# A bank of turned probabilities per job in both attention mixers of a two-block transformer kernel

## The chip, the cores and the metric

The kernel runs on one core of a Trainium2 chip. The metric is the device time of one execution in microseconds (us); lower is better. The engines named are TensorE (PE, matmuls; PEld is its weight loading), VectorE (DVE), ScalarE (ACT), GpSimd (POOL), and SyncE (SP), which issues the DMAs.

## The reference, cut to what matters

Two blocks of a transformer are computed one after the other on 256 tokens, in float32. The first block has two layers and carries 256 context tokens beside the 256 latent ones. Each layer is a half feed-forward, a mixer, and another half feed-forward. The change is in the two mixers of this first block, the "even" one (layer 0) and the "odd" one (layer 1).

```
# even mixer: 8 heads of latent attention beside a convolution of width 31 over 512 channels
att_c = context_attention(q_c, k_c, v_c)              # context queries over the 256 context keys
att_l = latent_attention(q_l, k_l, v_l, k_c, v_c)     # latent queries over context and latent keys, 512
y = a * sigmoid(g)                                    # for both token sets
y = depthwise_conv(y, width=31) + bias
y = layer_norm(y, g, b)                               # over the 512 channels
conv = silu(y)
out = concat([att, conv]) @ w_out

# odd mixer: 8 heads with 2 shared key heads, and 8 heads with a bias table by neighbourhood
s = q @ k.T * scale (+ bias)                          # 512 keys
p = softmax(s)
o = p @ v
```

## The kernel before, in words

The program is a list of blocks; in each, every engine has its own instruction stream, written out in order in the code, and semaphores (the tallies `t[...]`) join them. There is no scheduler: the order on an engine is the order of its Python code.

The attention of a mixer is a pipeline of 32 jobs. A job is one tile of 128 queries of one head; jobs 2h and 2h+1 are the two query tiles of head pair h. In `even_mixer` (line 1250) jobs 0 to 15 are the context's, over 256 keys, and jobs 16 to 31 the latents', over 512. In `odd_mixer` (line 1911) all have 512 keys; jobs 0 to 15 use the shared key heads and run between chunks of the input projection, jobs 16 to 31 add a bias by a second matmul. A job passes through these operations:

- `logits(j)` on PE (L1498; odd L2121, and L2130 with L2131 for the bias), into one of a few PSUM banks; it waits until `exponents` of the job that used the bank before is done.
- `maximum(j)` on DVE (L1811, L2315), `exponents(j)` on ACT (L1659, L2195), and on DVE `scaling_of(j)` (a reciprocal of the row sum, L1815, and a multiplication, L1817; odd L2302, L2304).
- `turn_probs(j)` on PE (L1507, L2098): transposes of the probabilities into PSUM, two for 256 keys, four for 512.
- a copy of the turned probabilities of both jobs of a pair from PSUM to SBUF. In the even mixer ACT makes it (`copy_probs`, L1666); over 512 keys a pair fills banks 4 and 5 together. In the odd mixer the pair always fills both banks, and ACT (`copy_even`, L2202) and DVE (`copy_odd`, L2311) copy half each.
- `weigh(h)` on PE (L1519, L2112), the product with the values, then `place(h)` on ACT (L1672, L2207).

The loop over slots sets the order. In slot s of the even mixer PE does turn_probs of job s-3, then weigh of a pair where one is due, then logits of job s. DVE does scaling_of job s-2, then maximum of job s, then some taps. ACT does the copy that is due, then exponents of job s.

The even mixer's convolution is 124 taps on DVE (L1778, one for each of 4 channel tiles and 31 positions), of which `TAPS_OF_UNIT` gives numbers to the seven units of the input projection and `TAPS_OF_STEP` to the steps of the loop. When all are done, its layer norm runs between the jobs: the mean over channels by four matmuls (L1567) in slot 16, its subtraction on DVE (L1872), the squares on ACT (L1737), the variance by 16 matmuls of one column (L1573) in slot 20, root on ACT (L1740) and reciprocal on DVE (L1875) on 4 columns, the spreading of the result over the partitions by four matmuls (L1579) in slot 22, the scaling on DVE (L1879), and the Silu on ACT (L1745) near the end. In two slots (`HEAD_AHEAD`) the first two weight units of the output projection are split into parts, ACT making the first (L511) and DVE the second (L519).

In the odd mixer SP loads tables of the bias in small pieces (L2001): those of heads 2 and 3 when the last norm of the input projection is done, those of heads 4 to 7 behind them and after the logits of job 15. DVE adds a mask to each (`mask`, L2298) at fixed steps, ahead of the scaling and maximum of that step.

After each mixer the output projection (L533) begins with parts of the mixed rows, split by ACT (L589) and DVE (L620).

## Time and profile before

| | us |
|---|---|
| median of 3 runs | 3458.52 (3452.37 to 3458.77) |
| the profiled execution | 3456.14 |
| its span | 3454.4 |
| PE busy in the span | 3246.7 (94%) |
| DVE busy | 1983.7 (57%) |
| ACT busy | 1410.2 (41%) |
| mean granted clock of TensorE | 0.969 of full speed |

The span is what the trace covers; the 1.7 us around it are start and end. Busy times are of one execution. Two matmuls in a row overlap at their ends, so the step from one start to the next is the cost of one, not the duration shown. float32 matmuls show as two rows each. A granted clock of 1.00 is 2.4 GHz, of 0.50 is 1.2 GHz.

### The profile page before, as it was taken

Reading aid. Unit: us, or ns where it says so; the run is one execution under the profiler, and the core shown is the slowest. Engines: PE = TensorE matmul, PEld = TensorE weight load, DVE = VectorE, ACT = ScalarE, POOL = GpSimd, SP = SyncE. Lnnn points to the kernel's source line nnn. Section 1 sums busy time; section 2 is a strip of 40 time slices with the busy share of each in tenths; the row PEclk is TensorE's granted clock in tenths of the full one; section 3 lists DMA queues with packets and bytes.
Section 4 is the critical chain, followed back from the end, with each engine's and each line's share of the span. In section 5 each row is a group of like instructions: output and inputs, shape, how many; then the busy total and the mean of one; then the engine's idle time right before and its main releaser. Section 6 shows DMA issues by size and latency. Waiting matters only on the chain. (4 is left out here: it accounts for less than half of the span.)

```text
span 3454.4 us, 51012 instructions
## 1 busy us (share of the span) xinstructions
PE 3246.7 (94%) x20326; PEld 2879.2 (83%) x20326; DVE 1983.7 (57%) x2557; ACT 1410.2 (41%) x2310; POOL 191.7 (6%) x151
## 2 busy tenths in 40 slices
PE   5999999789999999999889999999999999999999
PEld 4878777457787788887569999899999999999898
DVE  4776758537767733335555555566455555655654
ACT  3333335333333322224345444446444444454443
POOL 1000011000000100011000000200000102100000
PEclk8999999899999999999999999999999999999999
DMA  7566532015666433332226656554456565543564
GB/s 223 160 177 186 162 87 77 11 42 160 175 188 171 131 90 99 94 108 79 57 63 172 175 158 189 154 170 110 145 149 186 168 183 159 162 134 108 164 187 128
DMA packets 769419, 478.27 MB, mean 138 GB/s; under 512 B 37973, under 2 KB 746164, under 8 KB 769092
## 3 DMA queue, kind: packets, MB, share of 16 engines
q1 hardware_dynamic: 767200, 474.88, 48.5%
q8 instruction: 137, 2.24, 0.3%
q10 hardware_dynamic: 2020, 0.64, 0.1%
q14 instruction: 62, 0.51, 0.1%
HBM read 474.40 MB, written 1.05 MB: 138 GB/s over the span
## 5 line engine op out<-in xcount | busy, mean ns | idle before, releaser
L533 PE MATMUL psum<-normed,weights_part 128*128 128x256 f32 (+1 forms) x11616 | 1827.5, 319 | 39.5 <-DVE normed L808 11.6
L533 PEld LDWEIGHTS psum<-normed,weights_part 128*128 128x128 f32 x11616 | 1654.5, 193 | 197.3 <-issue 43.0
L519 DVE TENSOR_TENSOR weights_part<-weights,weights_part 128x2048 fp32r<-128x2048 f32 (+1 forms) x413 | 885.9, 2147 | 618.7 <-ACT weights_part L511 618.4
L511 ACT ACTIVATE weights_part<-weights 128x2048 fp32r<-128x2048 f32 (+1 forms) x413 | 738.5, 1791 | 654.3 <-PE psum L533 415.0
L533 PE MATMUL psum<-hidden,weights_part 128*128 128x256 f32 (+1 forms) x4224 | 680.7, 323 | 0.3 <-DVE hidden L821 0.3
L533 PEld LDWEIGHTS psum<-hidden,weights_part 128*128 128x128 f32 x4224 | 614.5, 190 | 61.8 <-DVE hidden L821 0.6
L1003 DVE SCALAR_TENSOR_TENSOR stage<-weights,cond,stage 128x768 f32<-128x768 f32 x294 | 281.1, 1020 | 0.0
L406 POOL TENSOR_TENSOR square<-square,rinvs 128x256 f32<-128x256 f32 (+1 forms) x39 | 65.1, 1669 | 2830.3 <-ACT rinvs L391 2828.7
L725 ACT ACTIVATE rinvs<-psum 128x256 f32<-128x256 f32 (+1 forms) x88 | 39.8, 452 | 210.6 <-PE psum L533 210.5
L533 PE MATMUL psum<-weights_part,normed 128*128 128x256 f32 x960 | 121.6, 287 | 0.0
L533 PEld LDWEIGHTS psum<-weights_part,normed 128*128 128x128 f32 x960 | 117.0, 192 | 4.9 <-issue 4.8
L727 ACT ACTIVATE hidden<-rinvs 128x256 f32 (+3 forms) x88 | 43.9, 499 | 177.0 <-DVE rinvs L819 177.0
L836 DVE SCALAR_TENSOR_TENSOR x<-psum,gate,x 128x256 f32<-128x256 f32 (+1 forms) x112 | 49.6, 479 | 113.2 <-PE psum L533 113.2
L727 ACT ACTIVATE hidden<-roots 128x256 f32 (+3 forms) x88 | 43.9, 499 | 173.0 <-DVE roots L819 173.0
L725 ACT ACTIVATE roots<-psum 128x256 f32<-128x256 f32 (+1 forms) x88 | 39.9, 454 | 177.6 <-PE psum L533 177.5
L819 DVE TENSOR_TENSOR rinvs<-rinvs,psum 128x256 f32<-128x256 f32 (+1 forms) x88 | 45.4, 516 | 97.2 <-ACT rinvs L725 97.2
L1778 DVE SCALAR_TENSOR_TENSOR mix<-ypad,vec,mix 128x512 f32<-128x512 f32 x120 | 87.1, 774 | 0.5
L819 DVE TENSOR_TENSOR roots<-roots,psum 128x256 f32<-128x256 f32 (+1 forms) x88 | 45.4, 516 | 63.5 <-ACT roots L725 63.5
L821 DVE TENSOR_TENSOR hidden<-rinvs,hidden 128x256 f32 (+3 forms) x88 | 46.3, 526 | 60.8 <-ACT hidden L727 60.8
L821 DVE TENSOR_TENSOR hidden<-roots,hidden 128x256 f32 (+3 forms) x88 | 46.3, 526 | 60.8 <-ACT hidden L727 60.8
L533 PE MATMUL psum<-mixed_part,weights_part 128*128 128x512 f32 (+1 forms) x384 | 70.1, 347 | 4.7 <-DVE mixed_part L620 4.7
L533 PEld LDWEIGHTS psum<-mixed_part,weights_part 128*128 128x128 f32 x384 | 61.7, 198 | 13.4 <-issue 5.6
(445 smaller groups left out, 2450.2 us busy)
## 6 DMA issues: line engine op xcount, KB each, us to landing
weights<-in_l_ffn_w_in SPq DMA_DIRECT2D x176, 512.0 KB, 5.2
weights<-in_ffn_w_gu SPq DMA_DIRECT2D x176, 512.0 KB, 4.9
weights<-in_l_mod_w SPq DMA_DIRECT2D x168, 384.0 KB, 3.4
weights<-in_w_in SPq DMA_DIRECT2D x34, 1024.0 KB, 5.2
weights<-in_w_gate SPq DMA_DIRECT2D x64, 512.0 KB, 5.2
weights<-in_l_ffn_w_out SPq DMA_DIRECT2D x64, 384.0 KB, 4.1
weights<-in_ffn_w_down SPq DMA_DIRECT2D x64, 384.0 KB, 3.9
weights<-in_l_ffn_w_out SPq DMA_DIRECT2D x64, 320.0 KB, 3.3
```

The costliest lines, as they stand in the source:

```text
L406: k.nc.gpsimd.tensor_tensor(total, total, buffers[n % 2], ALU.add).then_inc(summed.sem, 1)
L511: k.nc.scalar.activation(k.parts[part][0][:, W], k.slots[slot][:, W], ACT.Copy).then_inc(k.high_done, 1)
L519: k.nc.vector.tensor_tensor(k.parts[part][1][:, W], k.slots[slot][:, W], k.parts[part][0][:, W].bitcast(F32), ALU.subtract).then_inc(k.spl ...
L533: mm = k.nc.tensor.matmul(to, left[a], right[b], start=first and n == 0, stop=last and n == len(PASSES) - 1)
L725: nc.scalar.activation(row[:, T], k.psum[:, bank(spec, c), T], ACT.Silu).then_inc(t["silu_done"].sem, 1)
L727: nc.scalar.activation(one(k.hidden[0], i * RING + c, col=T), row[:, T], ACT.Copy)\
L819: nc.vector.tensor_tensor(row, row, k.psum[:, bank(spec, c) + 1, T], ALU.mult).then_inc(t["gated"].sem, 1)
L821: nc.vector.tensor_tensor(one(k.hidden[1], i * RING + c, col=T), row, one(k.hidden[0], i * RING + c, col=T).bitcast(F32), ALU.subtract)\
L836: last = nc.vector.scalar_tensor_tensor(row, k.psum[:, bank(spec, c), part], gate(chunk, cond) if callable(gate) else gate, row, ALU.mult, ...
L1003: ins = k.nc.vector.scalar_tensor_tensor(total, self.buffer(n), scale, total, ALU.mult, ALU.add)
L1778: last = nc.vector.scalar_tensor_tensor(total, of, weight, total, ALU.mult, ALU.add)
```

## The change

The pair of jobs no longer shares its copy. `turned_bank` takes a job: job j's turned probabilities go to bank 4 + j % 2, four tiles of 128 columns fill it exactly. `copy_probs(j)` on ACT copies one job's, in both mixers; the odd mixer's copy on DVE is gone. turn_probs(j) waits for the copy of job j-2. In a slot PE does the logits first, then turn_probs, then weigh; ACT does the copy, the exponents and only then `place`, a slot later than before. A slot is added at the end.

In the even mixer the taps are dealt anew: the units of the projection take 77 of the 124 (67 before), slots 0 to 2 two each and slots 3 to 15 one each (two each up to slot 14 before). The mean moves to slot 17, the variance to slot 22. The variance is now four matmuls of 512 columns against a matrix of 1/512, so that every partition gets it, and the spreading matmuls are gone; root (ACT) and reciprocal (DVE) work on 128x512 instead of 128x4, in slot 23. The Silus move behind the last exponents, and the two weight splits to slots 28 and 31.

```diff
-TAPS_OF_UNIT = (8, 10, 12, 11, 11, 13, 2)
-TAPS_OF_STEP = (2,) * HEAD_LOGITS + (2,) * 15
-CONV_MEAN, CONV_VARIANCE, CONV_SPREAD = 16, 20, 22
-HEAD_AHEAD = {24: 0, 27: 1}
+TAPS_OF_UNIT = (11, 13, 13, 13, 12, 13, 2)
+TAPS_OF_STEP = (2,) * (HEAD_LOGITS + 3) + (1,) * 16
+CONV_MEAN, CONV_VARIANCE, CONV_SCALED = 17, 22, 23
+HEAD_AHEAD = {28: 0, 31: 1}
...
-    def turned_bank(h):
-        if 2 * h < N_CONTEXT:
-            return k.psum[:, 4 + h % 2, :].rearrange("p (n q) -> p n q", q=LAT)
-        return k.psum[:, 4:6, :].rearrange("p b (n q) -> p (b n) q", q=LAT)
+    def turned_bank(j):
+        return k.psum[:, 4 + j % 2, :].rearrange("p (n q) -> p n q", q=P)[:, 0:len(key_tiles(j // 2)), :]
...
             def turn_probs(j):
                 pe.wait_ge(t["scaling"].sem, t["scaling"].base + j + 1)
-                h, qt = j // 2, j % 2
-                if qt == 0 and h:
-                    pe.wait_ge(t["copied"].sem, t["copied"].base + max(h - 1 if j < N_CONTEXT else h, 0))
...
+                if j >= 2:
+                    pe.wait_ge(t["copied"].sem, t["copied"].base + j - 1)
...
             def weigh(h):
-                pe.wait_ge(t["copied"].sem, t["copied"].base + h + 1)
+                pe.wait_ge(t["copied"].sem, t["copied"].base + 2 * h + 2)
...
+                if 0 <= s < N_HEAD_JOBS:
+                    logits(s)
...
                 for j in range(N_HEAD_JOBS):
                     if s == turn_slot(j):
                         turn_probs(j)
                 for h in range(N_HEAD_JOBS // 2):
                     if s == turn_slot(2 * h + 1) + 1:
                         weigh(h)
-                if 0 <= s < N_HEAD_JOBS:
-                    logits(s)
...
                 if s == CONV_VARIANCE:
-                    pe.wait_ge(t["conv_squared"].sem, t["conv_squared"].base + n_conv)
-                    for b in range(4):
-                        for c in range(n_conv):
-                            mm = nc.tensor.matmul(k.psum[:, 1, b:b + 1], conv_squares[c][:, b * P:(b + 1) * P], k.const("ones")[:, 0:1],
-                                                  start=c == 0, stop=c == n_conv - 1)
+                    for c in range(n_conv):
+                        pe.wait_ge(t["conv_squared"].sem, t["conv_squared"].base + c + 1)
+                        mm = nc.tensor.matmul(k.psum[:, 1, :], k.const("mean512"), conv_squares[c], start=c == 0, stop=c == n_conv - 1)
                     mm.then_inc(t["conv_variance"].sem, 1)
-                if s == CONV_SPREAD:
...
-            def copy_probs(h):
-                act.wait_ge(t["probs_turned"].sem, t["probs_turned"].base + 2 * h + 2)
+            def copy_probs(j):
+                h, qt = j // 2, j % 2
+                act.wait_ge(t["probs_turned"].sem, t["probs_turned"].base + j + 1)
                 if h >= 2:
                     act.wait_ge(t["weighted"].sem, t["weighted"].base + h - 1)
-                nc.scalar.activation(turned_probs[h % 2][:, 0:len(key_tiles(h)), :], turned_bank(h), ACT.Copy).then_inc(t["copied"].sem, 1)
+                nc.scalar.activation(turned_probs[h % 2][:, 0:len(key_tiles(h)), qt * P:(qt + 1) * P], turned_bank(j), ACT.Copy)\
+                    .then_inc(t["copied"].sem, 1)
...
+                if s >= N_HEAD_JOBS:
+                    for c in ((0,), (1, 2), (3,), (), ())[s - N_HEAD_JOBS]:
+                        gate_conv(c)
+            place(N_HEAD_JOBS // 2 - 1)
...
-                if s == CONV_VARIANCE + 1:
+                if s == CONV_SCALED:
                     dve.wait_ge(t["conv_root"].sem, t["conv_root"].base + 1)
-                    nc.vector.reciprocal(k.rms[:, 1, 0:4], k.rms[:, 0, 0:4]).then_inc(t["conv_inverse"].sem, 1)
+                    nc.vector.reciprocal(conv_inverse, conv_inverse).then_inc(t["conv_inverse"].sem, 1)
...
-            def copy_odd(h):
-                dve.wait_ge(t["probs_turned"].sem, t["probs_turned"].base + 2 * h + 2)
-                if h >= 2:
-                    dve.wait_ge(t["weighted"].sem, t["weighted"].base + h - 1)
-                nc.vector.tensor_copy(turned_probs[h % 2][:, 2:4, :], PT[:, 2:4, :]).then_inc(t["odd_copied"].sem, 1)
```

In the order of PE in the even mixer, from the variance on, before. Rows with `consts,weights` are turn_probs, with `head_rows` weigh, with `head_keys` logits; x4 counts calls.

```order
L1573 MATMUL psum<-consts,rinvs 128x1 x2
L1507 MATMUL psum<-consts,weights 128x128 x4
L1519 MATMUL psum<-head_rows_3953,head_values_3952 64x256 x4
L1498 MATMUL psum<-head_keys_3966,head_queries_3967 128x512
L1507 MATMUL psum<-consts,weights 128x128 x4
L1498 MATMUL psum<-head_keys_3966,head_queries_3967 128x512
L1579 MATMUL psum<-consts,rms 128x128 x4
L1507 MATMUL psum<-consts,weights 128x128 x4
```

The same place now:

```order
L1497 MATMUL psum<-head_keys_3966,head_queries_3967 128x512
L1505 MATMUL psum<-consts,weights 128x128 x4
L1570 MATMUL psum<-square,consts 128x512 x2
L1570 MATMUL psum<-rinvs,consts 128x512 x2
L1497 MATMUL psum<-head_keys_3966,head_queries_3967 128x512
L1505 MATMUL psum<-consts,weights 128x128 x4
L1517 MATMUL psum<-head_rows_3953,head_values_3952 64x256 x4
```

The logits of a slot now stand ahead of its transposes and of weigh, so a logits call stands between the copy of a pair and the weigh that needs it; the row of L1579 is gone.

On ACT in the even mixer around the root of the layer norm, before (`rinvs<-mix` is a square, `head_rows` the copy, `weights,head_rowsum` the exponents):

```order
L1659 ACTIVATE weights,head_rowsum_3964<-psum,head_negmax_3963 128x512
L1740 ACT_TABLE_LOAD
L1740 ACTIVATE rms<-psum,eps 128x4
L1666 ACTIVATE head_rows_3953<-psum 128x1024
L1659 ACT_TABLE_LOAD
L1659 ACTIVATE weights,head_rowsum_3964<-psum,head_negmax_3963 128x512
L1672 ACTIVATE mix_3950<-psum 64x256 x2
L1659 ACTIVATE weights,head_rowsum_3964<-psum,head_negmax_3963 128x512
```

Now:

```order
L1649 ACTIVATE weights,head_rowsum_3964<-psum,head_negmax_3963 128x512
L1737 ACT_TABLE_LOAD
L1737 ACTIVATE roots<-psum,eps 128x512
L1657 ACTIVATE head_rows_3953<-psum 128x4x128
L1649 ACT_TABLE_LOAD
L1649 ACTIVATE weights,head_rowsum_3964<-psum,head_negmax_3963 128x512
L1668 ACTIVATE mix_3950<-psum 64x256 x2
L1657 ACTIVATE head_rows_3953<-psum 128x4x128
```

A copy of 1024 columns for each pair has become one of 512 for each job, and the number of table loads at the root is the same.

On DVE in the odd mixer at the last masks, before (`odd_negmax` is the maximum, `weights` the scaling, `COPY` the copy of half a pair):

```order
L2298 TENSOR_TENSOR shared_queries_12105<-shared_queries_12105,consts 128x256 x2
L2302 RECIPROCAL odd_inverse_12115<-odd_rowsum_12114 128x1
L2304 TENSOR_SCALAR weights<-weights,odd_inverse_12115 128x512
L2311 COPY turned_probs_12111<-psum 128x512
L2315 TENSOR_REDUCE odd_negmax_12113<-psum 128x1
L2298 TENSOR_TENSOR shared_queries_12105<-shared_queries_12105,consts 128x256 x2
```

Now:

```order
L2296 TENSOR_TENSOR shared_queries_12152<-shared_queries_12152,consts 128x256 x2
L2300 RECIPROCAL odd_inverse_12162<-odd_rowsum_12161 128x1
L2302 TENSOR_SCALAR weights<-weights,odd_inverse_12162 128x512
L2307 TENSOR_REDUCE odd_negmax_12160<-psum 128x1
L2296 TENSOR_TENSOR shared_queries_12152<-shared_queries_12152,consts 128x256 x2
```

The copy between scaling and maximum is gone from DVE.

## Rows read from the trace of the kernel before

**Rows 1.** Windows: stretch, length; busy (count) of PE, PEld, DVE, ACT, POOL; PEclk, DMA, GB/s.

```profile
602.26:644.52 42.26, 29.23 (x96) 15.82 (x94) 34.58 (x79) 17.67 (x49) 0.23 (x1) 0.76 0.08 26
644.52:729.14 84.62, 60.97 (x219) 33.93 (x218) 30.63 (x63) 37.73 (x68) 0.00 (x0) 0.84 0.00 0
1622.61:1687.55 64.94, 64.54 (x394) 49.11 (x393) 33.35 (x52) 27.80 (x47) 0.00 (x0) 1.00 0.22 64
```

**Rows 2.** Timeline, PE, first mixer, 256 keys: start, duration, what, count, idle before and its releaser.

```profile
608.86 0.69 PE L1507 MATMUL psum<-consts,weights 128*128 128x128 f32 x2 [4.25 <-DVE weights L1817]
...
619.50 1.08 PE L1519 MATMUL psum<-head_rows,head_values 128*64 128x256 f32 x4
620.51 0.70 PE L1498 MATMUL psum<-head_keys,head_queries 96*128 96x256 f32 x2
```

**Rows 3.** Timeline of DVE, first mixer, the same jobs.

```profile
610.84 0.42 DVE L1811 TENSOR_REDUCE head_negmax<-psum 128x1 f32<-128x256 f32 x1
611.17 1.41 DVE L1778 SCALAR_TENSOR_TENSOR mix<-ypad,vec,mix 128x512 f32<-128x512 f32 x2
...
612.95 0.42 DVE L1811 TENSOR_REDUCE head_negmax<-psum 128x1 f32<-128x256 f32 x1
```

**Rows 4.** Timeline of PE, first mixer, jobs over 512 keys and the end.

```profile
644.52 3.60 PE L1567 MATMUL psum<-mix,consts 128*128 128x512 f32 x8
...
659.99 0.61 PE L1573 MATMUL psum<-consts,square 128*128 128x1 f32 x4 [2.91 <-ACT rinvs L1737]
...
703.90 1.12 PE L1507 MATMUL psum<-consts,weights 128*128 128x128 f32 x4 [5.02 <-DVE weights L1817]
...
729.14 6.17 PE L533 MATMUL psum<-mixed_part,weights_part 128*128 128x512 f32 x19 [2.60 <-DVE mixed_part L620]
```

**Rows 5.** Timeline of ACT, second mixer: root, tables.

```profile
1649.51 0.60 ACT L2177 ACTIVATE near_values<-psum 128x512 f32<-128x512 f32 x1 [1.37 <-PE psum L533]
1650.12 1.28 ACT L2189 ACT_TABLE_LOAD   x1
1651.42 0.69 ACT L2189 ACTIVATE rinvs<-psum,eps 128x512 f32<-128x512 f32 x1
```

**Rows 6.** Timeline of DVE, second mixer: reciprocal of a whole tile.

```profile
1652.27 3.34 DVE L2263 RECIPROCAL rinvs<-rinvs 128x512 f32<-128x512 f32 x1
```

**Rows 7.** Timeline of PE, second mixer: one pair of jobs late in its loop.

```profile
1735.05 0.63 PE L2098 MATMUL psum<-consts,weights 128*128 128x128 f32 x4 [0.40 <-ACT turned_probs L2202]
1735.61 1.94 PE L2112 MATMUL psum<-turned_probs,near_values 128*64 128x256 f32 x8
1737.48 1.13 PE L2130 MATMUL psum<-near_keys,near_queries 128*128 128x512 f32 x2
...
1738.87 0.60 PE L2098 MATMUL psum<-consts,weights 128*128 128x128 f32 x4
1739.31 1.02 PE L2130 MATMUL psum<-near_keys,near_queries 128*128 128x512 f32 x2
1740.17 0.59 PE L2131 MATMUL psum<-shared_queries,consts 128*128 128x256 f32 x2
1741.16 0.63 PE L2098 MATMUL psum<-consts,weights 128*128 128x128 f32 x4 [0.40 <-ACT stage L2202]
```

**Rows 8.** Timeline of SP and DVE, second mixer: the bias tables.

```profile
1688.15 0.69 DVE L2311 COPY stage<-psum 128x512 f32<-128x512 f32 x1
...
1693.09 10.35 SPq L2001 DMA_DIRECT2D roots<-in_l_na_rpb  x16
...
1716.69 0.76 DVE L2298 TENSOR_TENSOR shared_queries<-shared_queries,consts 128x256 f32<-128x256 f32 x2 [5.60 <-DMA shared_queries<-in_l_na_rpb]
```

**Rows 9.** Timeline of PE, second mixer: after the bias wait, and the end.

```profile
1718.10 1.12 PE L2098 MATMUL psum<-consts,weights 128*128 128x128 f32 x4 [6.01 <-DVE weights L2304]
...
1767.49 17.77 PE L533 MATMUL psum<-mixed_part,weights_part 128*128 128x256 f32 x134 [2.12 <-DVE mixed_part L620]
```

**Rows 10.** Timeline of DVE, first mixer: taps before a weight split.

```profile
519.68 2.29 DVE L519 TENSOR_TENSOR weights_part<-weights,weights_part 128x2048 fp32r<-128x2048 f32 x1 [1.89 <-ACT weights_part L511]
```

More of the change, by code:

```diff
@@ L1299, in even_mixer @@
     tap_before = {(c, n): tap_place[c, n - 1] for c, n in TAPS if n}
-    slots = HEAD_LOGITS + N_HEAD_JOBS + HEAD_LAG + 1
+    conv_inverse = k.roots[:, 0, :]
+    slots = HEAD_LOGITS + N_HEAD_JOBS + HEAD_LAG + 2
     def bank_rows(u):
@@ L1552, in _ @@
                     head_step(f)
+                if 0 <= s < N_HEAD_JOBS:
+                    logits(s)
+                for g in range(len(GROUPS)):
+                    if f == TURNED_AT[g]:
+                        turn_group(g)
                 for j in range(N_HEAD_JOBS):
@@ L1558, in _ @@
                         weigh(h)
-                if 0 <= s < N_HEAD_JOBS:
-                    logits(s)
-                for g in range(len(GROUPS)):
-                    if f == TURNED_AT[g]:
-                        turn_group(g)
                 if s == CONV_MEAN:
@@ L1724, in _ @@
                         evict_group(n)
-                for h in range(N_HEAD_JOBS // 2):
-                    if s == turn_slot(2 * h + 1):
-                        copy_probs(h)
-                    if s == turn_slot(2 * h + 1) + 1 and h % 2:
-                        place(h)
+                for j in range(N_HEAD_JOBS):
+                    if s == turn_slot(j):
+                        copy_probs(j)
                 if 0 <= s < N_HEAD_JOBS:
                     exponents(s)
+                for h in range(1, N_HEAD_JOBS // 2, 2):
+                    if s == turn_slot(2 * h + 1) + 2 and h < N_HEAD_JOBS // 2 - 1:
+                        place(h)
                 if s in HEAD_AHEAD:
@@ L1943, in odd_mixer @@
     chunks = {FIRST_CHUNK + n: chunk for n, chunk in enumerate(CHUNKS)}
[L1944 removed]
+    last_step = FIRST_LOGITS + turn_slot(N_JOBS - 1) + 2
     parts_of_tokens = halves(TOK)
@@ L1986, in head, with turned_bank @@
         return (j % N_SHARED) // 2
-    PT, O = k.psum[:, 4:6, :].rearrange("p b (n q) -> p (b n) q", q=LAT), k.psum[:, 6, :]
+    def turned_bank(j):
+        return k.psum[:, 4 + j % 2, :].rearrange("p (n q) -> p n q", q=P)
+    O = k.psum[:, 6, :]
     spread_bank = (4, 5, 6, 7, 7, 7, 7, 7, 7)
@@ L2157, in _ @@
                         turn_heads(g)
+                if 0 <= s < N_JOBS:
+                    logits(s)
                 for j in range(N_JOBS):
@@ L2163, in _ @@
                         weigh(h)
-                if 0 <= s < N_JOBS:
-                    logits(s)
         @block.scalar
@@ L2242, in _ @@
                     root(ROOTS_AT[f])
-                for h in range(N_JOBS // 2):
-                    if s == turn_slot(2 * h + 1):
-                        copy_even(h)
-                    if s == turn_slot(2 * h + 1) + 1 and h % 2:
-                        place(h)
+                for j in range(N_JOBS):
+                    if s == turn_slot(j):
+                        copy_probs(j)
                 if 0 <= s < N_JOBS:
                     exponents(s)
+                for h in range(1, N_JOBS // 2, 2):
+                    if s == turn_slot(2 * h + 1) + 2:
+                        place(h)
         @block.vector
@@ L2359, in _ @@
                         scaling_of(j)
-                for h in range(N_JOBS // 2):
-                    if s == turn_slot(2 * h + 1):
-                        copy_odd(h)
                 if 0 <= s < N_JOBS:
```

62 lines of the change are left out of this document (26 added, 36 removed).

## The prediction

> **What bounds the kernel now.** I read the page first. PE is busy 94% of the span, so only places where PE waits or runs at a low clock can give much. The 40 slices show two such places, at the ends of the two attention loops, and the windows around them give the sizes. In the first mixer PE is busy 29.23 us of 42.26 while the context's jobs run, at a mean clock of 0.76, and 60.97 of 84.62 us in the rest, at 0.84 [rows 1]. A mean of 0.76 is 1.2 GHz for about half of the stretch. The early part of the second mixer is another case: PE busy 64.54 of 64.94 us at full clock, covered by the projection's chunks. There the order inside a slot is worth nothing. What ends PE's waits stands in the timelines. At the start it waits 4.25 us for the first scaling, behind DVE's taps [rows 2]. DVE takes 2.11 us from one maximum to the next, with two taps that last 1.41 together [rows 3]. Over 512 keys PE waits for the squares of the layer norm, 2.91 us, and for a scaling queued behind a weight split, 5.02 us [rows 4]. Late in the second mixer every pair shows a 0.40 us wait for a copy, and 6.11 us from pair to pair [rows 7]; once, PE waits 6.01 us, because DVE waits 5.60 us for bias tables [rows 8, 9]. Neither ACT nor DVE is full over 512 keys (37.73 and 30.63 of 84.62 us [rows 1]). Both loops end in a chain to the output projection, which starts at 729.14 and 1767.49 [rows 4, 9], and what follows is mostly PE, so I let a shift of these two starts count fully.
>
> **Prices at full clock**, start to start: logits over 512 keys 0.86, four transposes 0.44, weigh over 512 keys 1.87, bias matmul half of the logits, 0.43 [rows 7]; weigh over 256 keys 1.01 [rows 2]. Logits and transposes over 256 keys I take as half, 0.43 and 0.22.
>
> **First mixer, projection.** Ten taps move into the units, at 0.7 us (half of 1.41 [rows 3]) 7 us. Before the weight split DVE stands idle, 1.89 us at the third unit [rows 10], and no unit gets more than three taps more, 2.1 us. PE needs that split only a unit later. Cost 0; without that cover at most the 7 us.
>
> **First mixer, context jobs.** The start stays: the first scaling still stands behind the same taps, and the maximum of job 3 stays at 610.84 [rows 3]. From slot 3 on DVE has one tap: 2.11 - 0.7 = 1.4, I take 1.45 us a slot. PE needs 0.43 + 0.22 + 0.5 = 1.2 at full clock, 2.4 at half. At full clock DVE sets the pace and the maximum of job 16 is at 610.84 + 13 x 1.45 = 629.7; at half clock PE does, 13 x 2.4 = 31.2, at 642.0. I assume one cold spell of about 3.5 slots at the start, since the 4.25 us wait remains: 3.5 x 0.95 = 3.3, so 633.0, logits of job 16 at 632.3.
>
> **First mixer, jobs over 512 keys.** With the copy made a slot ahead of its weigh, and two banks, PE should run without the copy's waits. ACT needs for a job about 0.7 for the exponents, 0.6 for the copy and 0.4 for place, less than PE's 2.24 (0.86 + 0.44 + 0.94). Sum on PE for slots 16 to 27: 12 logits 10.3, transposes of jobs 13 to 24 4.6, weigh 6 to 11 9.5, mean and variance 8 matmuls of 0.86 6.9, and 0.1 a slot for gaps 1.2: 32.5. To this comes one new wait. Counted from the logits of job 22, the variance ends at 4.7, the exponents of job 23 at 7.4, table load 1.28 and root 0.69 [rows 5] 9.4, and the reciprocal of a whole tile takes 3.34 [rows 6] where 4 columns took almost nothing: 12.8. The scaling of job 22 stands behind it on DVE and is done at 13.3; PE comes to its transposes at 10.1. It waits 3.2. Together 35.7. Bounds of this wait: 0 if PE is late anyway, 5 if the root is.
> Slots 28 to 35: 4 logits 3.4, 7 turns 3.1, 4 weighs 7.5, so 14.0. The split in slot 28 lasts 1.9 on ACT and 2.29 on DVE [rows 10] and holds the next scaling; PE has one slot of slack and waits 1.9. The one in slot 31 holds the scaling of job 30 with fewer jobs left to cover it: 4.4 (5.02 before [rows 4]). The last copy before the last weigh 0.7. Together 21.0. Moving the Silus costs nothing: three of them and their table load, about 3.2 us of ACT, lie beside the 4.4 wait.
> For cold PE after the waits of 3.2 and 4.4 I add 2.5 + 3.0. The last weigh ends at 632.3 + 35.7 + 21.0 + 5.5 = 694.5, and the projection starts 2.6 later [rows 4], at 697.1 instead of 729.14: -32.0. The removed parts (the wait of 2.91, 16 small matmuls, the spreading and its wait) are within this difference.
>
> Where the page's rule would change this: the row shows a table load of 1.28 behind an ACT instruction that has just ended, and the root starting 1.30 after the load's start [rows 5]. The Trainium skill, page "ScalarE: Activation LUTs", section "What ACT_TABLE_LOAD costs", says that a switch costs the load and then a drain of about 1.38 us, 2.66 in all. By that rule the reciprocal would end 1.4 later and the wait be 4.6 instead of 3.2. The trace does not agree, so the sum keeps 1.28.
>
> **Second mixer.** Until 1687.55 nothing. Then DVE does one copy fewer (0.69, 0.6 net [rows 8]) ahead of the last norm, after which SP issues the bias tables at 1693.09; their landing, 23.6 later at 1716.69, holds DVE, and through it PE until 1718.10 [rows 8, 9]. So this point moves by 0.6 only, to 1717.5, whatever PE does before it. One logits call is moved ahead of the wait. After it: transposes of 15 jobs 6.6, 11 logits with bias 14.2, 8 weighs 15.0, together 35.8, 0.3 of gaps, 0.9 for the last copy, 2.5 for a cold start as before: 39.5. The last weigh ends at 1757.0, the projection starts 2.1 later at 1759.1, against 1767.49: -8.4. Bounds: nothing gained beyond the 0.6, or 2.5 more if the start is warm.
>
> **Sum.** 32.0 + 8.4 = 40.4. 3456.14 - 40.4 = 3415.7 for the profiled execution, which lies 2.4 below the median of the runs shown and inside their spread. I forecast 3416.
>
> **Rivals.**
> 1. Same mechanism, warmer: PE is so dense that it stays at 2.4 GHz through both loops. Then 3.3 + 5.5 + 2.5 fall away: 3405. For it: late in the second mixer PE kept full clock in a loop with a 0.40 us wait per pair. Against it: the waits of 4.25 and 6.0 us remain [rows 2, 9], and the clock fell with such: four transposes last 1.12 behind the 6.01 wait, 0.63 elsewhere [rows 7, 9].
> 2. New waits take half of it: the layer norm's chain (variance, root, 3.34 us reciprocal) and the splits each stall the in-order DVE and ACT longer than I worked out, since ACT's copy now stands ahead of every exponents and itself waits for PE's transposes. Price: some 8 us more in the full-key part, 4 to 5 us of cold PE with it, and the context jobs at 638 rather than 633: 3416 + 17 = 3433. For it: half of PE's waits before were for scaling on DVE [rows 2, 4]. Against it: three slots lie between exponents and transposes.
> 3. Slower: the clock. If short gaps at every bank change keep TensorE at 1.2 GHz through both loops, the context jobs end at 642.0; the work after them, 32.5 + 14.0 = 46.5, takes 93 with the splits hidden, so the projection starts at 738, 9 later than now; the second mixer's 35.8 take 72, and its projection starts 25 later. Together 3490. It decides when about half of the some 100 us of PE work in the loops runs at 1.2 GHz beyond what I assumed, as each such microsecond costs one more. Against it: the mean clock in the sparser loop of now is 0.76 and 0.84 [rows 1], not 0.5.
> The Trainium skill, page "TensorE: Matmul & The Clock Gate", section "A second HAM failure mode: psum-queue depth-cycling", tells of this: cycling through PSUM banks every iteration gives PE small idle times between groups, and its clock goes back and forth. The rows late in the second mixer, gaps of 0.40 without such a fall, speak against it here.
> 4. It does not do what it says: the waits for copies were only a cover for DVE's pace, and PE now waits for scaling instead, with the reciprocal's 3.34 and the later tail paying the rest back: 3456. For it: DVE's 34.58 busy of 42.26 us in the context part [rows 1]. Against it: the taps removed there are DVE's.
>
> **Chances.** The forecast 0.58 (its own range 3409 to 3426), rival 1 0.15, rival 2 0.21, rival 3 0.04, rival 4 0.02. The range 3403 to 3438 takes in rivals 1 and 2 nearly whole and the bounds of the new waits. A measurement of this kernel can tell 0.2%, 7 us, from no change. Faster by more than that holds in the first three cases, 0.94; slower in rival 3, 0.04; within it in rival 4, 0.02.
>
> **What would show it.** Right: maxima in slots 3 to 15 of the first mixer about 1.45 us apart once the clock is up; PE busy over 80% from job 16 on, no wait of transposes for a copy, a wait of about 3 us behind the 128x512 reciprocal and one of about 4 behind the second split; the projections starting near 697 and 1727 (1759 less the 32 before); a pair in the second mixer every 5.3 to 5.5 us; the bias landing still the longest wait there. Wrong: PEclk near 0.5 through the loops, scaling waits of several us per pair, or PE waiting for weight splits in the first mixer's projection.

## The result

| | before | after |
|---|---|---|
| median, us (lowest to highest) | 3456.1 (3452.4 to 3458.8), 4 runs | 3420.5 (3417.3 to 3425.9), 4 runs |
| ratio, 95% interval | | 0.9899 (0.988 to 0.9918) |
| profiled execution, its span | 3456.14, 3454.4 | 3425.85, 3424.1 |

The changed kernel is 1% faster. Its profiled execution is the slowest of its four, so stretches are compared below, not spans. The first fence has the windows of the changed kernel that answer to [rows 1]: the context jobs, the jobs over 512 keys with the way to the projection, and the second mixer from turn(17) to its projection.

```profile
607.29:636.50 29.21, 25.59 (x104) 14.57 (x102) 27.21 (x71) 18.70 (x58) 0.00 (x0) 0.88 0.11 37
636.50:698.66 62.16, 49.55 (x179) 25.84 (x179) 31.62 (x59) 38.32 (x76) 0.00 (x0) 0.92 0.00 0
1687.32:1731.91 44.59, 40.03 (x169) 24.11 (x169) 19.21 (x49) 22.07 (x55) 0.00 (x0) 0.94 0.00 1
```

The context jobs take 29.21 us instead of 42.26, the next stretch 62.16 instead of 84.62, the last 44.59 instead of the 49.39 between the two rows of [rows 9]. PE is busy 88% and 80% of the first two, and its mean clock rose from 0.76 and 0.84 to 0.88 and 0.92. The timeline of DVE, over 256 keys, answers to [rows 3]:

```profile
624.35 0.42 DVE L1807 TENSOR_REDUCE head_negmax<-psum 128x1 f32<-128x256 f32 x1
624.68 0.74 DVE L1774 SCALAR_TENSOR_TENSOR mix<-ypad,vec,mix 128x512 f32<-128x512 f32 x1
...
625.80 0.41 DVE L1807 TENSOR_REDUCE head_negmax<-psum 128x1 f32<-128x256 f32 x1
```

One tap stands between two maxima that are 1.45 us apart, not two and 2.11. The timeline of PE over 512 keys answers to [rows 4]:

```profile
661.77 1.01 PE L1505 MATMUL psum<-consts,weights 128*128 128x128 f32 x4 [3.06 <-DVE weights L1813]
...
678.96 1.12 PE L1505 MATMUL psum<-consts,weights 128*128 128x128 f32 x4 [2.64 <-DVE weights L1813]
...
688.66 0.66 PE L1505 MATMUL psum<-consts,weights 128*128 128x128 f32 x4 [3.62 <-DVE weights L1813]
...
694.12 1.94 PE L1517 MATMUL psum<-head_rows,head_values 128*64 128x256 f32 x8 [0.69 <-ACT head_rows L1657]
...
698.66 0.70 PE L533 MATMUL psum<-mixed_part,weights_part 128*128 128x512 f32 x2 [2.60 <-DVE mixed_part L620]
```

Three waits for a scaling are left, behind the reciprocal and behind each weight split; no transposes wait for a copy. In the second mixer, what answers to [rows 7, 9]:

```profile
1687.32 1.12 PE L2095 MATMUL psum<-consts,weights 128*128 128x128 f32 x4 [7.87 <-DVE weights L2302]
...
1697.77 1.94 PE L2108 MATMUL psum<-stage,near_values 128*64 128x256 f32 x8
...
1703.74 1.91 PE L2108 MATMUL psum<-turned_probs,near_values 128*64 128x256 f32 x8 [0.38 <-ACT x L2204]
...
1709.23 1.94 PE L2108 MATMUL psum<-stage,near_values 128*64 128x256 f32 x8
...
1724.66 1.91 PE L2108 MATMUL psum<-turned_probs,near_values 128*64 128x256 f32 x8 [1.00 <-ACT x L2204]
...
1731.91 0.36 PE L533 MATMUL psum<-mixed_part,weights_part 128*128 128x256 f32 x1 [2.12 <-DVE mixed_part L620]
```

From weigh to weigh it is 5.97 and 5.49 us in turn, against 6.11 before. Each longer one holds a wait that was not there before, for ACT's `place`.

**Where the time went, by stretches.** A runs from the first head step to the layer norm's mean, B from there to the first mixer's output projection, C from the last spreading of the second mixer (1657.05, before 1687.55) to its projection. Each length is the difference of two starts on PE. The last four kernels come from the experiments.

| kernel | A | B | C | median, us | ratio to before (95%) |
|---|---|---|---|---|---|
| before | 80.01 | 84.62 | 79.94 | | |
| after | 68.84 | 62.16 | 74.86 | 3420.5 | 0.9899 (0.988 to 0.9918) |
| first mixer only | 68.79 | 62.13 | 79.91 | 3428.9 | 0.9921 (0.9905 to 0.9938) |
| second mixer only | 78.26 | 83.03 | 74.54 | 3447.9 | 0.9984 (0.9973 to 0.9995) |
| before, logits first | 72.91 | 74.54 | 74.94 | 3435.8 | 0.9944 (0.9929 to 0.9959) |
| after, logits last | 74.53 | 72.53 | 80.49 | 3444.0 | 0.9968 (0.9958 to 0.9978) |

Before and after differ by 38.7 us in these three stretches (11.2, 22.5, 5.1). What lies outside them differs by chance: the mixer starts at 483.53 instead of 480.36 in code that is the same, and in the fourteen kernels profiled for this text that start lies between 477.3 and 483.5; between the first projection and the last spreading it is 958.4 us in both; from the second projection to the end it is 1685 to 1696 us in all of them (1686.9 before, 1692.2 after).

How far can one trace be trusted for one stretch? The changed code repeats well: in the four kernels that have its first mixer unaltered, A is 68.52 to 68.84 and B 61.87 to 62.16, and in the seven with its second mixer C is 74.54 to 74.92. The old first mixer was traced twice and repeats less well: the second-mixer kernel, which has it too, shows A and B 1.75 and 1.6 shorter than before. Measured against that trace, the gain of the first mixer is 30.3 us and not 33.6, and that of the three stretches 35.4 and not 38.7, which is nearer to the 35.6 between the medians. So gains counted from before in A and B may be some 2 us too large in each; differences between changed kernels are not touched by this.

### The profile page after: what moved, and what is told of

It is laid out like the page before. It is cut to its first block and busy times, and to the rows that moved or that the text cites. A ratio compares the mean times of both kernels' runs of the same rounds, so it can differ in the third digit from the quotient of the medians.

```text
span 3424.1 us, 51000 instructions
## 1 busy us (share of the span) xinstructions
PE 3239.0 (95%) x20294; PEld 2878.2 (84%) x20294; DVE 1977.5 (58%) x2541; ACT 1420.1 (41%) x2342; POOL 193.0 (6%) x151
```

## The experiments

Medians in one set of runs are compared with before in the same set (3454.4, 3458.5, 3454.1, 3453.5); the ratios account for that, so two kernels of different sets are compared by their ratios (0.001 is 3.5 us). Stretches are those of the table.

**1. The two mixers apart.** The diff's part on one mixer was taken, that on the other left out.

> Only the second mixer's part of the change, on the kernel before. Theory (the two mixers' gains add, each where the two traces show it): the first mixer is as before (84.6 us from its mean to the output projection), the second mixer's stretch from turn(17) to its projection takes 44.6 us instead of 49.4, and the time is 5 us below before, near 3451. Rival (part of the second mixer's gain comes from what the first mixer's change leaves behind, or from nothing but the shift of a run): less than 2 us.

> Only the first mixer's part of the change: the second mixer as before. Theory: the output projection of the first mixer starts 30 to 34 us earlier than before, the second mixer keeps its pairs of 6.11 us and 49.4 us from turn(17) to its projection; the time is 31 us below before, near 3425, that is 5 us above the changed kernel. Rival: the second mixer's part cost something elsewhere and this kernel is as fast as the changed one, 3420.

Measured: 0.9984 and 0.9921, whose product is 0.9905 against 0.9899 for both. From turn(17) to the projection 44.75 us with the second mixer's part alone; with the first mixer's alone its A and B are those of the changed kernel within 0.05 and C that of before. The gains add, and the first mixer has 33.6 of 38.7 us. The time of the first-mixer kernel, 3428.9, is above the 3425 that I expected: by its ratio it is 27 us below before (21 to 33), where I expected 31. That fits the 30.3 us of the other trace of the old first mixer better than the 33.6.

**2. The taps.**

```
-TAPS_OF_UNIT = (11, 13, 13, 13, 12, 13, 2)
-TAPS_OF_STEP = (2,) * (HEAD_LOGITS + 3) + (1,) * 16
+TAPS_OF_UNIT = (8, 10, 12, 11, 11, 13, 2)
+TAPS_OF_STEP = (2,) * HEAD_LOGITS + (2,) * 15
```

with the old order of `TAPS`.

> The changed kernel with the old dealing of the taps (8, 10, 12, 11, 11, 13, 2 in the units, two in each of 29 steps). Theory (VectorE's two taps of 1.41 us set the pace of the context slots, 2.11 us against 1.45): slots 0 to 14 are 0.66 us longer, 10 us in all, time near 3430; the seven units before the heads start no earlier. Rival A (the taps moved into the units cost there what they save later): near 3420, and the first logits start earlier than in the changed kernel by several us. Rival B (the PE's cold clock in the context slots is the bound): under 3 us.

Measured: 3424.7, ratio 0.991 (0.9894 to 0.9927); A 75.10 instead of 68.84, B and C the same (62.03, 74.55). So the taps are worth 6.3 us in the trace, not 10; the two ratios, whose intervals overlap, do not show it. I had counted 15 slots of 0.66 us, but only ten taps were moved (77 instead of 67 in the units), and a slot pays 0.66 for each: 6.6. Rival A falls: from the first unit to the first head step it is 84.16 us here and 84.13 with the taps in the units. Rival B falls with the 6.3.

**3. The order in a slot, and the banks.** First the changed kernel with `logits(s)` issued behind `turn_probs` and `weigh` again:

> The changed kernel, with the logits of a slot issued last, behind the transposes and the weighing, in both mixers, as before the change. Theory (the bank per job is what gives the gain; the order in a slot is worth little because a job's probabilities are turned three slots after its logits): 2 to 4 us slower than the changed kernel, 3422 to 3425, pairs of full jobs still 5.5 to 6 us. Rival (the order carries the gain: with logits last VectorE's maximum comes behind the weighing, and the transposes wait for the scaling): 8 us or more slower, 3429 or more, with waits of PE for the scaled probabilities in each pair.

Measured: 3444.0, 24 us slower; my theory falls. Everything that the change gave in C and half of what it gave in A and B is gone, though each job has its own bank. The timeline of this kernel over 256 keys, two engines, shows the ring:

```profile
618.50 0.44 PE L1505 MATMUL psum<-consts,weights 128*128 128x128 f32 x2 [0.57 <-DVE weights L1813]
...
618.87 1.08 PE L1517 MATMUL psum<-head_rows,head_values 128*64 128x256 f32 x4
...
619.87 0.70 PE L1497 MATMUL psum<-head_keys,head_queries 96*128 96x256 f32 x2
...
620.61 0.43 DVE L1807 TENSOR_REDUCE head_negmax<-psum 128x1 f32<-128x256 f32 x1 [0.71 <-PE psum L1497]
```

The transposes wait for DVE's scaling, the logits stand behind transposes and weigh, the maximum waits 0.71 us for the logits, and the next scaling stands behind the maximum. The pair takes 3.71 us, not 2.90. In the second mixer of the same kernel the weigh waits for `place`, which stands behind exponents that wait for these late logits:

```profile
1723.37 1.91 PE L2108 MATMUL psum<-turned_probs,near_values 128*64 128x256 f32 x8 [1.91 <-ACT x L2204]
```

So part of this loss is a meeting of the old order on PE with the new one on ACT; how large a part was not measured, and the clean test of the order is the last one of this group. Next, the changed kernel with the first mixer's two banks shared by a head's two jobs, as before, and one copy a head:

```
-                if j >= 2:
-                    pe.wait_ge(t["copied"].sem, t["copied"].base + j - 1)
+                if qt == 0 and h:
+                    pe.wait_ge(t["copied"].sem, t["copied"].base + max(h - 1 if j < N_CONTEXT else h, 0))
```

(with `turned_bank` and `copy_probs` of before).

> The changed kernel with the first mixer's two PSUM banks shared by a head's two jobs again, copied once for both by ACT alone (logits stay first, taps and layer norm as changed, second mixer as changed). Theory (the first transposes of a full head wait for the copy of the head before, as in the kernel before): full pairs of 16 to 31 are longer by 1.5 to 2.5 us each, eight pairs: 12 to 20 us, time 3432 to 3440; the context slots keep 1.45 us. Rival (logits first alone fills PE while the copy runs): under 5 us, 3425 or less.

Measured: 3423.9, ratio 0.9907 (0.9889 to 0.9924); A 68.54, B 62.75, C 74.79. The rival holds: waits for the copy come back, but three of 0.34 us only, and the last of 0.69 becomes 1.11, since the logits of the slot run in front of them. The banks of the second mixer were not tested alone; the next kernel bears on them. Last, the kernel before with nothing but the logits moved first, in both mixers:

> The kernel before with one edit: in both mixers a slot's logits are issued ahead of the transposes and the weighing, and nothing else of the change (two jobs' probabilities still share their banks, VectorE still copies half in the second mixer, old taps, old layer norm, old slots of the splits). Theory now, after the changed kernel with logits last came out 24 us slower and the one with shared banks 3 us (the order carries the gain; a bank per job alone gives nothing): first mixer from the mean to the projection under 74 us instead of 84.6 and its context jobs 4 to 5 us shorter, second mixer 75 to 76 us from spread(8) to the projection instead of 79.9; time 3436 to 3442. Rival (each part covers for the other: with shared banks and late copies in place the order alone gives under 5 us, and only the two together give the gain): 3450 or more.

Measured: 3435.8, ratio 0.9944 (0.9929 to 0.9959). A is 7.1 us shorter than before, B 10.1, C 5.0, together 22 of the 38.7 (by the ratio 19, from 14 to 25). In B I had expected more (under 74 us), in the context jobs less (4 to 5 us, not 7.1). In C that is all that the change gave. The kernel with everything but the order gained 17.0 in the three stretches; 22.2 and 17.0 are 39.2, so the order and the rest nearly add.

How the order gives the 7.1 in A stands on DVE, before:

```profile
616.87 0.42 DVE L1811 TENSOR_REDUCE head_negmax<-psum 128x1 f32<-128x256 f32 x1 [1.71 <-PE psum L1498]
...
627.02 0.43 DVE L1811 TENSOR_REDUCE head_negmax<-psum 128x1 f32<-128x256 f32 x1 [1.45 <-PE psum L1498]
...
637.50 0.42 DVE L1811 TENSOR_REDUCE head_negmax<-psum 128x1 f32<-128x256 f32 x1 [1.40 <-PE psum L1498]
```

With those at 642.73 (1.45) and 644.72 (1.10) they are five waits of DVE for logits, 7.1 us in sum; the first four are for logits that stood right behind a weigh on PE. In the kernel with the order alone only one of 0.35 is left. So the pace before was not the 2.11 us of [rows 3]: from the maximum of job 3 to that of job 16 it took 33.9 us, 2.6 a slot.

The weighs of its second mixer, with the two banks shared and DVE still copying half, on PE:

```profile
1716.49 1.94 PE L2112 MATMUL psum<-turned_probs,near_values 128*64 128x256 f32 x8
...
1722.02 1.94 PE L2112 MATMUL psum<-stage,near_values 128*64 128x256 f32 x8
...
1727.54 1.94 PE L2112 MATMUL psum<-turned_probs,near_values 128*64 128x256 f32 x8
```

A pair takes 5.52 us. In the changed kernel, which has a bank per job, it is 5.97 and 5.49 in turn, 5.73 in the mean.

**4. The layer norm.** First its old form in the new slots: the variance by 16 products of one column in slot 22, root and reciprocal of four columns in 23, the spreading in 24.

> The changed kernel with the layer norm's old form (16 products of one column for the variance, root and reciprocal of 4 columns, then the spreading), in the slots of the new one (variance 22, root 23, spreading 24). Theory (the two forms cost about the same: the 16 small products take 6.8 us on PE in the trace of the kernel with the order alone, against 3.4 for the products over 512 columns, and leave a cold PE behind; against that stand the 3.06 us wait behind the whole reciprocal and the cold PE behind it): first mixer from the mean to the projection 61 to 64 us instead of 62.2, time 3419 to 3422. Rival A (the new form is a real part of the gain: the small products, their root's turn around and the spreading are all on PE's path): 66 us or more, 3425. Rival B (the reciprocal's stall is the dearer): 59 us or less, 3417.

Measured: 3419.3, ratio 0.9899 (0.9882 to 0.9915), B 61.43 against 62.16. The theory holds: the two forms cost the same here. What the small products do is in the windows of this kernel, of the sixteen products in two parts and of the jobs behind them:

```profile
643.58:645.36 1.78, 1.78 (x18) 1.78 (x17) 1.01 (x3) 1.27 (x3) 0.00 (x0) 1.00 0.03 9
645.36:648.78 3.42, 3.42 (x18) 3.42 (x18) 0.00 (x0) 0.00 (x0) 0.00 (x0) 0.50 0.00 0
648.78:651.62 2.84, 2.84 (x8) 1.37 (x8) 0.69 (x1) 0.00 (x0) 0.00 (x0) 0.50 0.00 0
```

PE is busy all the time, and the clock is at 2.4 GHz, then at 1.2. (A busy PE is one with a matmul on record; the ends of matmuls are modelled.) Second, the new form with its reciprocal in four parts:

```
-                if s == CONV_SCALED:
+                if CONV_SCALED < s <= CONV_SCALED + 4:
+                    part = conv_inverse[:, (s - CONV_SCALED - 1) * P:(s - CONV_SCALED) * P]
...
-                if CONV_SCALED < s <= CONV_SCALED + n_conv:
+                if CONV_NORMED < s <= CONV_NORMED + n_conv:
```

with CONV_NORMED = 27.

> The changed kernel with the layer norm's reciprocal of 128x512 cut into four of 128x128, one in each of slots 24 to 27, and the four products by it in slots 28 to 31. Theory (PE waits 3.06 us behind the whole reciprocal, and its clock falls behind the wait): the wait goes, projection 3 to 5 us earlier in its stretch of 62.2 us, time near 3416. Rival (VectorE's queue is full enough that the four pieces delay the scaled probabilities as much in sum, or the products moved to the splits' slots lengthen the waits there): no gain, 3419 to 3422.

Measured: 3419.1, ratio 0.9887 (0.9871 to 0.9904), B 58.68: 3.5 us shorter, as the theory has it. DVE has room for a part in each slot, and PE's waits behind the splits grow:

```profile
656.02 0.69 DVE L1807 TENSOR_REDUCE head_negmax<-psum 128x1 f32<-128x512 f32 x1 [2.08 <-PE psum L1497]
656.63 0.94 DVE L1872 RECIPROCAL roots<-roots 128x128 f32<-128x128 f32 x1
```

```profile
673.28 0.66 PE L1505 MATMUL psum<-consts,weights 128*128 128x128 f32 x4 [3.30 <-DVE weights L1813]
...
683.78 0.85 PE L1505 MATMUL psum<-consts,weights 128*128 128x128 f32 x4 [4.44 <-DVE weights L1813]
```

The wait of 3.06 is gone, and 2.64 and 3.62 became 3.30 and 4.44: the products moved to the splits' slots take back 1.5, as the rival said. By the ratios the kernel is 4 us below the changed one, but the two intervals overlap; the 3.5 are shown by the trace alone.

**5. The weight splits.** DVE's half of a split one slot behind ACT's half.

```
-                if s in HEAD_AHEAD:
-                    split_low(k, dve, 0, out.start + HEAD_AHEAD[s])
+                if s - 1 in HEAD_AHEAD:
+                    split_low(k, dve, 0, out.start + HEAD_AHEAD[s - 1])
```

> The changed kernel with VectorE's half of both weight splits one slot behind ScalarE's half (29 and 32 instead of 28 and 31). Theory (VectorE stands 3.63 and 3.21 us for ScalarE's half with the scaled probabilities of a job behind it in its queue; PE waits 2.64 and 3.62 us for them): VectorE no longer waits, only its own 2.29 us stays, PE's two waits shrink by 1.5 to 2 each, time 3 to 4 us lower, near 3417. Rival (ScalarE's 1.91 us delays the exponents as much, so that PE waits the same): within 1 us of 3420.

Measured: 3414.5, ratio 0.9875 (0.9859 to 0.9892), B 58.17, 4.0 us shorter. DVE and PE of this kernel, around the first split:

```profile
671.47 2.29 DVE L519 TENSOR_TENSOR weights_part<-weights,weights_part 128x2048 fp32r<-128x2048 f32 x1 [2.34 <-ACT weights_part L511]
```

```profile
674.41 0.66 PE L1505 MATMUL psum<-consts,weights 128*128 128x128 f32 x4 [1.34 <-DVE weights L1813]
...
679.30 0.86 PE L1517 MATMUL psum<-head_rows,head_values 128*64 128x256 f32 x3 [1.34 <-ACT head_rows L1657]
```

PE waits 1.34 us instead of 2.64. At the second split it waits 0.49 instead of 3.62 for the scaling. Part of this comes back as waits for ACT's copies, 1.34 and 1.79 us, where the changed kernel has one of 0.69. I was wrong in one detail: DVE still stands 2.34 us before its half, but one more job has been scaled in front of it, so the scaling that stands behind it is needed later.

**6. The second mixer's waits.** The masks of the last four heads later:

```
-MASKED_AT = (18, 20, 23, 24, 25, 26, 27, 28)
+MASKED_AT = (18, 20, 23, 24, 28, 29, 32, 33)
...
-pe.wait_ge(t["masked"].sem, t["masked"].base + (4, 8, 16, 16)[h // 2])
+pe.wait_ge(t["masked"].sem, t["masked"].base + (4, 8, 12, 16)[h // 2])
```

> The changed kernel, second mixer: the masks of the last four heads, which wait for the last bias DMAs, come at steps 28, 29, 32 and 33 instead of 25 to 28, and the logits of heads 4 and 5 wait for 12 masks instead of 16. Theory (PE's 7.87 us before turn(17) are VectorE's, which waits for the bias to land with the scaled probabilities of job 17 behind it): that wait falls to under 2 us, some of it comes back before job 24 (whose logits need the bias that lands near 1684): 5 to 8 us lower, 3412 to 3415. Rival (the wait only moves to job 24's logits): within 1.5 us of 3420.

Measured: 3414.4, ratio 0.9869 (0.9852 to 0.9885), C 64.95 instead of 74.86. The wait of 7.87 us is gone from PE, and with it the cold stretch behind it, so 9.9 us in the trace (10 by the ratios), more than the wait and more than the 5 to 8 that I expected. DVE still waits for the landing, but three jobs later, with enough logits scored in front:

```profile
1678.94 0.69 DVE L2307 TENSOR_REDUCE odd_negmax<-psum 128x1 f32<-128x512 f32 x1 [0.20 <-PE psum L2127]
1683.49 0.76 DVE L2296 TENSOR_TENSOR shared_queries<-shared_queries,consts 128x256 f32<-128x256 f32 x2 [3.86 <-DMA shared_queries<-in_l_na_rpb]
```

```profile
1684.90 0.66 PE L2095 MATMUL psum<-consts,weights 128*128 128x128 f32 x4 [0.48 <-DVE weights L2302]
```

And two banks in turn for the weighted sums of the last eight heads:

```
-    O = k.psum[:, 6, :]
+    def weighted_bank(h):
+        return k.psum[:, 7 if h >= HEADS and h // 2 % 2 else 6, :]
```

> The changed kernel with two PSUM banks in turn for the weighted sums of the second mixer's last eight heads. Theory (each second pair's weighing waits 0.37 to 1.00 us for ScalarE's place, which now comes behind the exponents, and the pair takes 5.97 instead of 5.49): the waits go, all pairs 5.49, 2 us lower, 3418. Rival (ScalarE's place delays the copies just the same): under 0.5 us in the second mixer.

Measured: 3415.4, ratio 0.9892 (0.9877 to 0.9907), C 73.00 instead of 74.86; between weighs 5.52 and 5.53 us, and no wait for `place`. The 1.9 us are in the trace; the ratio alone would not tell it from the changed kernel.

**7. The four edits together,** reciprocal in parts, masks later, two banks, and DVE's halves of the splits in slots 29 and 33 (the second one behind the last scaling).

> The changed kernel with all four: the layer norm's reciprocal in four parts (slots 24 to 27, products in 28 to 31), VectorE's halves of the weight splits in slots 29 and 33, the masks of the last four heads later, two banks for the last weighted sums. Theory (the waits are separate, their prices add): first mixer from the mean to the projection 54 us or less instead of 62.2, second mixer from spread(8) to the projection 63 instead of 74.9: 20 us below the changed kernel, near 3400. Rival (the products of the layer norm in the splits' slots and the split itself meet on VectorE, and the first mixer keeps 58): 3405.

Measured: 3400.8 (3395.6 to 3407.7), ratio 0.985 (0.9837 to 0.9863): 19.7 us under the changed kernel by the medians, 17 by the ratios, the fastest of all. Its windows, of A without the head steps, of B and of C:

```profile
599.41:629.99 30.58, 25.27 (x103) 14.39 (x102) 28.82 (x73) 18.80 (x58) 0.23 (x1) 0.89 0.11 35
629.99:684.64 54.65, 47.34 (x180) 24.77 (x179) 31.55 (x62) 38.08 (x76) 0.00 (x0) 0.94 0.00 0
1643.07:1706.08 63.01, 57.34 (x238) 33.11 (x239) 32.83 (x78) 30.32 (x75) 0.00 (x0) 0.97 0.17 36
```

B is 7.5 shorter than in the changed kernel (3.5 and 4.0 apart), C 11.9 (9.9 and 1.9 apart): the prices add, down to 0.1 us, though the second split's half stands one slot later here. PE is busy 87% of B and 91% of C.

## Why the prediction held, step by step

**Taps into the units: cost 0.** Right: from the first unit to the first head step 84.13 us, before 84.15. DVE's idle time before the third split is gone, as the cover was meant to be used; the row answers to [rows 10]:

```profile
522.83 2.29 DVE L519 TENSOR_TENSOR weights_part<-weights,weights_part 128x2048 fp32r<-128x2048 f32 x1
```

**Context jobs: 1.45 us a slot, one cold spell of 3.3.** The pace is exact. From the maximum of job 3 to that of job 16 it is 20.24 us; 13 slots by 1.45 leave 1.4 for the cold spell. So from the first head step to the logits of job 16 it took 65.5 us where I had 67.8. What I gave as the reason was only half of it: the taps are worth 6.3 (experiment 2); order and the rest must give the other 5 of A's 11.2, and the order alone gave 7.1 on the old kernel. I built the new pace from DVE's own work; that the maxima would no longer wait for late logits, 7.1 us of the time before (experiment 3), was in the sum without a word. Nor did the wait of 4.25 us remain, which I took as the cause of the cold spell. With the logits issued first it is two shorter ones, the first of them

```profile
612.19 0.44 PE L1505 MATMUL psum<-consts,weights 128*128 128x128 f32 x2 [1.41 <-DVE weights L1813]
```

and 1.37 before the next transposes, behind which PE ran at 1.2 GHz all the same (0.69 for the same transposes).

**Jobs over 512 keys: waits of 3.2, 1.9, 4.4 and 0.7.** Measured 3.06, 2.64, 3.62 and 0.69. PE is busy 79.7% of B, just short of the 80 that I had named as a sign. From the logits of job 16 (633.13) to the projection 65.5 us, where I had 64.8. The root that ended the first of these waits, on ACT, and the reciprocal on DVE:

```profile
655.80 1.28 ACT L1737 ACT_TABLE_LOAD   x1
657.09 0.69 ACT L1737 ACTIVATE roots<-psum,eps 128x512 f32<-128x512 f32 x1
```

```profile
657.81 3.35 DVE L1871 RECIPROCAL roots<-roots 128x512 f32<-128x512 f32 x1 [3.05 <-ACT roots L1737]
```

The root starts 1.29 us after its table load, as in [rows 5]. By the drain of 1.38 that the Trainium skill has (page "ScalarE: Activation LUTs", section "What ACT_TABLE_LOAD costs") it would start 2.66 after it; the trace does not agree here either.

The sum of the first mixer was −32.0; measured −33.6 (164.63 to 131.00 us from the first head step to the projection; −30.3 with the other trace of the old code). But the step "with the copy made a slot ahead of its weigh, and two banks, PE should run without the copy's waits" put the gain in the wrong place. With shared banks it stays within 0.6 us (experiment 3); the logits moved ahead of a wait, which I priced only once and in the second mixer ("one logits call is moved ahead of the wait"), are what carries it: 17 of the 33.6 in the first mixer with nothing else changed. Of the other 12.4 us in B the bank is 0.6, the taps 0.1 and the norm's form none (−0.7). The rest, some 12 us and so nearly a third of the whole gain, can only lie in what was moved by slots (variance two later, splits four later, Silus apart, `place` behind the exponents) or in how these act together; that is by elimination and not shown. In the kernel with the order alone the squares are still waited for 2.80 us and the last copies 2.09 and 1.60; I have not run these moves apart.

**Second mixer: −8.4.** Measured −5.1, the term that was off most, by 3.3 us. The bias landing stayed the longest wait, and the point after it moved by 0.28 us (30.27 against 30.55 from the last spreading), not 0.6: the first of the bias DMAs is issued 0.6 earlier, but sixteen take 10.85 us to issue, against 10.35 in [rows 8]; why, no run tells. The SP queue and DVE:

```profile
1661.98 10.85 SPq L2000 DMA_DIRECT2D roots<-in_l_na_rpb  x16
```

```profile
1685.91 0.76 DVE L2296 TENSOR_TENSOR shared_queries<-shared_queries,consts 128x256 f32<-128x256 f32 x2 [7.87 <-DMA shared_queries<-in_l_na_rpb]
```

From turn(17) to the end of the last weigh it is 42.5 us where I had 39.5. Of these 3.0 us, 1.75 are waits for `place` (0.38, 0.37, 1.00). The change put it behind the exponents of its slot, on one bank, and my sum has no line for it; two banks take 1.9 off C, and 1.3 of them off this part. The cold start cost 2.75, not 2.5 (the first 6.79 us hold work that is 4.04 at full clock: 0.44, 0.86, 0.43, 0.44, 1.87), and a clean pair 5.49 is at the upper end of 5.3 to 5.5.

**The sum.** −38.7 us in the three stretches against −40.4. The profiled execution is only 30.3 below that of before, because 3.2 us in front of the mixer and 5.3 behind the second projection went the other way by chance; the medians are 35.6 apart, 5 us less than the 40.4 of the forecast, and 3420.5 stands in the forecast's own range. The three stretches come within 1.7 us of the forecast in part by luck: the way to the logits of job 16 was 2.3 shorter than forecast, from there to the projection it was 0.7 longer, and the second mixer gained 3.3 less.

**The rivals.** Rival 1 (warm all through) did not come: cold PE stood behind each long wait. Of rival 2 one new wait came true, in the second mixer, worth 1.75 of its 17. Rival 3 did not: the mean clock rose in the first mixer (0.76 and 0.84 to 0.88 and 0.92) and is 0.91 in C before and after. What the Trainium skill says of this on the page "TensorE: Matmul & The Clock Gate", section "A second HAM failure mode: psum-queue depth-cycling", finds nothing here: with a new bank for each job and with shared banks the mean clock of B is 0.92 in both. Rival 4 fell with the 38.7.

## What to carry to other kernels

In a loop over several in-order engines, issue what the longest chain starts with (here the logits) ahead of what waits for that chain's end; that one swap gave 22 us in the trace of the old kernel (19 by the ratio); with it in place, separate banks in the first mixer gave less than one. Before a wait is priced, look at what is queued behind it: masks moved by three to five slots, so that enough work stood in front of them, took off 9.9 us where the wait was 7.87, as the cold clock behind it went too. And compare kernels stretch by stretch, since a gain of 2 us in a stretch does not show in the median; but trace the kernel before more than once, for here its two traces differ by 1.75 and 1.6 us in the two stretches that gained most.

## What the chip showed that I had not expected

In one trace the clock fell while PE was never idle, neither then nor in the 10.58 us before, all at 1.00: during sixteen products of one column it went from 1.00 to 0.50, with 3.42 of 3.42 us busy, and four matmul records went from 0.445 us to 0.855 (experiment 4). So products with one column save little: the sixteen took 5.2 us (643.58 to 648.78), against 3.4 in the changed kernel for the four of 512 columns (649.58 to 653.01), and what follows them ran at 1.2 GHz for another 2.84 us. The Trainium skill, page "TensorE: Matmul & The Clock Gate", section "HAM oscillation — how this bites in real kernels", speaks of the clock falling after gaps in which PE is idle; here there is no gap.

The same wait did not always end in the same clock. With the new taps PE waits 2.11 us for the key rows' eviction near the end of the head steps, before 1.91. In the changed kernel, and in the one with its first mixer only, the clock then fell, in the other kernels with the same wait it did not. PE of the changed kernel, and of the one with the later splits:

```profile
600.41 1.86 PE L1483 MATMUL psum<-consts,head_rows 128*96 128x128 f32 x8 [2.11 <-ACT head_keys L1633]
602.06 2.79 PE L1466 MATMUL psum<-weights,mix 128*128 128x512 f32 x4
```

```profile
596.27 1.05 PE L1483 MATMUL psum<-consts,head_rows 128*96 128x128 f32 x8 [2.11 <-ACT head_keys L1633]
597.15 1.88 PE L1466 MATMUL psum<-weights,mix 128*128 128x512 f32 x4
```

It cost 1.65 us there (39.6 against 37.95 from the first head step to the first logits), and 1.4 of them came back in the context jobs, which took 29.2 instead of 30.6.
